# Expert results summed in PSUM, with one buffer for the rows of a block that VectorE transposes

## The chip, the cores and the metric

The kernel runs on one core of a Trainium2 chip, in float32. The metric is device time in microseconds (us) of one execution, the median of three runs.

## The reference

Two trunk layers, each a mixer (layer 0: retention and differential attention; layer 1: a Hyena convolution) followed by a mixture of experts, work on 384 tokens of 1024 channels (128 context tokens and 256 latent tokens). What matters here is the mixture of experts and the sum behind it:

```python
def moe_ffn(h, router_w, router_bias, w_gate, w_up, w_down):    # 16 experts, D_FF_EXPERT = 512
    scores = sigmoid(t @ router_w)                              # t: the tokens
    ...
    _, eidx = lax.top_k(jnp.where(emask, sel, -jnp.inf), TOP_K) # TOP_K = 2
    wsel = jnp.take_along_axis(scores, eidx, axis=-1)
    wsel = wsel / wsel.sum(-1, keepdims=True)
    ...
    act = jax.nn.silu(hg) * hu * comb[:, :, None].astype(t.dtype)
    return jnp.einsum('tef,efd->td', act, w_down).reshape(B, L, D)
...
    h = x * (1.0 + sc2) + sh2
    y = moe_ffn(h, ...)
    x = layer_norm(ALPHA * x + g2 * y, P['ln_w'][l, 1], P['ln_b'][l, 1])
```

## The kernel before

The 384 tokens are three tiles of 128. The router gives each token two experts, and each of the 768 pairs gets a slot. The slots of an expert fill blocks of 32 slot rows, so that an expert has one block or more; how many is known only at run time. GpSimd scatters the tokens' rows (1024 float32 each) into a table in DRAM, `slot_rows`, with six indirect DMAs.

A loop then goes over the 16 experts (`pe_moe`, experts with many and with few blocks mixed) and over each expert's blocks (`block_of_expert`). SyncE's queue streams the weights, three transfers of 2 MB for each expert (gate, up, down), in the order of the experts, into four pairs of buffers for gate and up and three for down; a buffer is filled again when the last block of its expert has read it. With two layers these are 96 transfers.

One block is this, by engine:

- TensorE: `gate_and_up` for eight groups of 128 channels (L954; the slot rows, transposed, are the stationary operand of 32 columns, and four matmuls fill the four groups of 32 columns of the array), then `rows_to_channels` (L947: four transposes of the **next** block's rows), then `down` for four groups of 128 hidden units (L961), which waits until VectorE has delivered the gated and transposed activation.
- ScalarE: silu of the gate (L1409); half of the down result from PSUM to SBUF (L1412), the other half by VectorE (L1546); then ScalarE's queue stores the block to `slot_rows` in two DMAs (L1417).
- VectorE: silu times up and the transpose, in two halves (L1529, L1531), the next block's rows from PSUM (L1524), the copy (L1546).
- GpSimd: it waits until the rows have landed in `slot_ahead[odd]` and until TensorE has transposed the last ones, copies them to `slot_in` (L575, L576) and issues the reads of the block after next into the buffer that has just come free (L566), two DMAs of 32 x 512 float32.

The first two blocks of a layer don't come from DRAM: a matmul with a 0/1 matrix picks them out of the tokens.

After the loop GpSimd gathers two rows for each token from `slot_rows` with six indirect DMAs, TensorE multiplies them by diagonal matrices of the routing weights and adds them (`pe_join` in layer 0, `pe_last` in layer 1), and VectorE adds the gated sum to the residual (`total`, in `dve_norm` and `dve_last`) and takes the statistics of the layer norm (L1286 and L1339). In layer 0 the matmuls of the next modulation (L633) stand ahead of the join on TensorE, and SyncE's first load of the Hyena weights waits for the gathers.

## Time and profile before

| | |
|---|---|
| runs | 1202.0, 1203.97 and 1207.95 us, median 1203.97 us |
| profiled execution | 1201.09 us, of which the span of the trace is 1199.4 us |
| mean granted TensorE clock | 0.951 |
| busy share of the span | PE 84%, PEld 47%, DVE 33%, ACT 20%, POOL 16% |
| read from and written to HBM | 320.02 MB, 23.63 MB |
| chain of work that ended last | PE 63%, DMA 21%, DVE 10% |

The span is the time from the first to the last instruction of the trace; the execution's own time has a little more around it. PE is TensorE's matmuls, PEld its loads of stationary operands, which run beside them; DVE is VectorE, ACT ScalarE, POOL GpSimd, and SP SyncE. The granted clock is a share of 2.4 GHz. In rows of the trace L954 is line 954 of the kernel, and "[0.54 <-DVE arena L1531]" means that the engine had been idle for 0.54 us until an instruction of VectorE at L1531 released it. A float32 matmul leaves two records, so 32 matmuls of `gate_and_up` appear as x64.

### The profile page before, as it was taken

To read this page: it belongs to the slowest core of one execution; us is meant where nothing else is said; L and a number is where in the kernel's file an instruction comes from. 1 tells how busy PE (TensorE), PEld (TensorE's weight loads), DVE (VectorE), ACT (ScalarE), POOL (GpSimd) and SP (SyncE) were. 2 spreads that over 40 slices of the span, in tenths; PEclk is the share of its full clock that TensorE was granted. 3 is DMA by queue.
4 is the path that set the end of the run, shared out by engine and by line. 5 is a ranking of instruction groups with operands and counts; after the bars stand their busy time and mean duration, and the time that the engine had idled before them with its cause. 6 is when DMAs were issued, how large, how long until landed. Compare 5 with 4: busy or idle time off the path is not lost.

```text
span 1199.4 us, 24149 instructions
## 1 busy us (share of the span) xinstructions
PE 1013.1 (84%) x9499; PEld 561.7 (47%) x9499; DVE 400.3 (33%) x1149; ACT 239.8 (20%) x507; POOL 190.9 (16%) x389
## 2 busy tenths in 40 slices
PE   4899998899769899795679999999978977998564
PEld 2344447654435455453345555455454544555231
DVE  0320115744612222121353533645552221222116
ACT  0401003631411121111131111210141121121102
POOL 0320000300032222122110001002004221222111
PEclk9999999899789999898889999999979998999988
DMA  8998232977589999999892314636765799899984
GB/s 354 324 343 299 95 126 97 350 298 317 222 302 396 388 407 393 397 399 394 305 377 99 140 71 143 243 123 241 292 256 211 270 391 408 337 395 393 394 349 158
DMA packets 76278, 344.62 MB, mean 287 GB/s; under 512 B 8883, under 2 KB 9011, under 8 KB 62900
## 3 DMA queue, kind: packets, MB, share of 16 engines
q1 hardware_dynamic: 54756, 291.40, 62.9%
q0 software_dynamic: 14512, 41.78, 10.2%
q10 hardware_dynamic: 6944, 10.49, 2.5%
q8 instruction: 49, 0.80, 0.3%
q14 instruction: 17, 0.14, 0.0%
HBM read 320.02 MB, written 23.63 MB: 287 GB/s over the span
## 4 chain that ended last, share of the span: by engine, by line
PE 63%; DMA 21%; DVE 10%; ACT 2%; issue 2%; SPq 1%; POOL 0%; POOLq 0%; ACTq 0%; DVEq 0%
PE bank L954 13%; PE bank L743 12%; PE bank L1019 11%; PE bank L961 7%; DMA ring<-in_moe_w_up_dram 7%; PE bank L872 7%; DMA ring<-in_ada_w_dram 3%; DMA ring<-in_moe_w_down_dram 3%; DMA arena<-in_moe_w_up_dram 3%; PE bank L633 3%; DMA ring<-in_ev_w_in_dram 3%; PE bank L1122 1%; PE bank L1098 1%; ACT arena L1409 1%; DVE arena L1531 1%
## 5 line engine op out<-in xcount | busy, mean ns | idle before, releaser
L954 PE MATMUL bank<-ring,arena 128*32 128x256 f32 x2496 | 149.9, 391 | 28.8 <-DMA ring<-in_moe_w_up_dram 25.7
L743 PE MATMUL bank<-ring,arena 128*128 128x512 f32 x336 | 146.7, 598 | 2.5 <-DMA ring<-in_ev_w_in_dram 2.5
L954 PE MATMUL bank<-arena 128*32 128x256 f32 x1792 | 108.1, 395 | 28.3 <-DMA arena<-in_moe_w_up_dram 28.3
L1019 PE MATMUL bank<-arena,ring 128*128 128x384 f32 x384 | 126.3, 492 | 1.9 <-issue 1.9
L1529 DVE TENSOR_TENSOR arena<-arena,bank 128x64 f32<-128x64 f32 x136 | 27.4, 201 | 296.2 <-ACT arena L1409 296.2
L954 PEld LDWEIGHTS bank<-ring,arena 128*32 128x32 f32 x2496 | 83.7, 113 | 88.5 <-issue 41.7
L961 PE MATMUL bank<-ring,arena 128*32 128x256 f32 x1440 | 87.0, 382 | 27.3 <-DVE arena L1531 22.2
L743 PEld LDWEIGHTS bank<-ring,arena 128*128 128x128 f32 x336 | 64.2, 192 | 82.9 <-issue 80.2
L1019 PEld LDWEIGHTS bank<-arena,ring 128*128 128x128 f32 x384 | 73.5, 192 | 54.4 <-issue 5.0
L954 PEld LDWEIGHTS bank<-arena 128*32 128x32 f32 x1792 | 60.3, 114 | 72.0 <-issue 39.4
L872 PE MATMUL bank<-ring,arena 128*128 128x512 f32 x192 | 83.2, 593 | 1.3 <-DVE arena L2096 1.3
L566 POOL DMA_DIRECT2D arena<-slot_rows x140 | 70.8, 506 | 60.6 <-POOL arena L576 43.5
L961 PEld LDWEIGHTS bank<-ring,arena 128*32 128x32 f32 x1440 | 42.9, 109 | 55.9 <-DVE arena L1531 33.2
L1412 ACT ACTIVATE arena<-bank 64x256 f32<-64x256 f32 x68 | 25.9, 381 | 181.8 <-PE bank L961 181.8
L1546 DVE COPY arena<-bank 64x256 f32<-64x256 f32 x68 | 28.3, 416 | 100.1 <-PE bank L961 100.1
L575 POOL TENSOR_TENSOR small<-small 128x1 f32<-128x1 f32 x66 | 12.4, 188 | 298.5 <-PE bank L947 291.5
L872 PEld LDWEIGHTS bank<-ring,arena 128*128 128x128 f32 x192 | 36.2, 190 | 45.7 <-issue 44.0
L1409 ACT ACTIVATE arena<-bank 128x128 f32<-128x128 f32 x68 | 18.8, 277 | 186.9 <-PE bank L954 185.7
L961 PE MATMUL bank<-arena 128*32 128x256 f32 x704 | 42.5, 382 | 14.3 <-DVE arena L1531 11.1
L1409 ACT ACT_TABLE_LOAD x34 | 43.6, 1283 | 47.2 <-issue 47.2
L633 PE MATMUL bank<-ring,small 128*32 128x256 f32 x640 | 39.4, 402 | 9.5 <-DMA ring<-in_ada_w_dram 9.5
L576 POOL COPY arena<-arena 64x512 f32<-64x512 f32 x66 | 39.6, 600 | 0.0
(367 smaller groups left out, 1074.9 us busy)
## 6 DMA issues: line engine op xcount, KB each, us to landing
ring<-in_ada_w_dram SPq DMA_DIRECT2D x24, 2048.0 KB, 13.4
ring<-in_moe_w_down_dram SPq DMA_DIRECT2D x20, 2048.0 KB, 23.5
ring<-in_moe_w_gate_dram SPq DMA_DIRECT2D x18, 2048.0 KB, 24.1
ring<-in_moe_w_up_dram SPq DMA_DIRECT2D x18, 2048.0 KB, 29.4
arena<-in_moe_w_gate_dram SPq DMA_DIRECT2D x14, 2048.0 KB, 26.7
arena<-in_moe_w_up_dram SPq DMA_DIRECT2D x14, 2048.0 KB, 31.9
arena<-in_moe_w_down_dram SPq DMA_DIRECT2D x12, 2048.0 KB, 20.1
ring<-in_ev_w_in_dram SPq DMA_DIRECT2D x7, 2048.0 KB, 19.4
```

What stands on the lines that cost most here:

```text
L566: pool.dma_start(slot_ahead[odd][h * BLK:(h + 1) * BLK, :], slots[bass.ds(block * BLK, BLK), h * 512:(h + 1) * 512]).then_inc(S[f"row_in{o ...
L576: pool.tensor_copy(slot_in, slot_ahead[odd]).then_inc(S["row_rdy"], 1)
L633: pe.matmul(b[32 * j:32 * j + 32, 0:HALF], condT[:, 2 * k:2 * k + 32], slot8(chunks[j // 2])[:, k, j % 2 * HALF:j % 2 * HALF + HALF], star ...
L743: last = pe.matmul(bank[3 * (c % 2) + t], hT[:, k, t * P:(t + 1) * P], slot8(n)[:, k, :], start=k == 0, stop=k == KT - 1)
L872: last = pe.matmul(bank[2 * t + half], src[:, k, t * P:(t + 1) * P], slot8(n0 + half)[:, k, :], start=k == 0, stop=k == KT - 1)
L954: last = pe.matmul(bank[1][q * BLK:(q + 1) * BLK, 0:HALF], slot_inT[:, k, :], both[:, :, k, q * P:(q + 1) * P], start=k == 0, stop=k == KT ...
L961: last = pe.matmul(bank[5][tile * BLK:(tile + 1) * BLK, 0:HALF], act_T[:, f, :], slot4(s + 2)[:, f, q * HALF:(q + 1) * HALF], start=f == 0 ...
L1019: last = pe.matmul(bank[c % 3][:, 0:T], slot8(n)[:, k, (c % 4) * P:(c % 4 + 1) * P], hT[:, k, :], start=k == 0, stop=k == KT - 1)
L1409: act.activation(silu_g, bank[1][:, 0:P].rearrange("p (r f) -> p f r", f=FT), ACT.Silu).then_inc(S["silu"], 1)
L1412: act.activation(slot_out[odd][:, HALF:2 * HALF], bank[5][2 * BLK:4 * BLK, 0:HALF], ACT.Copy).then_inc(S["evac_act"], 1)
L1529: dve.tensor_tensor(act_rows[:, two, :], silu_g[:, two, :], up, ALU.mult).then_inc(S["gated"], 1)
L1546: dve.tensor_copy(slot_out[odd][:, 0:HALF], bank[5][0:2 * BLK, 0:HALF]).then_inc(S["evac_dve"], 1)
```

## The change

The down results no longer go to DRAM. Six of the eight PSUM banks hold the sum for all 384 tokens and 1024 channels during the whole loop. After each block, twelve matmuls (`add_to_tokens`, three tiles of tokens by four quarters of the channels) add its 32 rows to the tokens they belong to. Their stationary operand `sel_w` is 32 slot rows by 128 tokens and holds the routing weight where the token has that slot, and 0 elsewhere; it is laid out four times, once for each group of 32 rows of the array, and VectorE makes it anew for each block from the tokens' slots and weights, which are spread over the partitions once per layer. The stores, the gathers, the diagonal matrices and the joining matmuls go, and so do some matmuls (`WARM`, `LAST_WARM`) whose result nobody read.

The rows of a block are read by one DMA of 32 x 1024 float32 into the one buffer `slot_ahead`. VectorE, not TensorE, transposes them, with four instructions of 32 x 256, and GpSimd issues the next read when these are done. The loops of VectorE, ScalarE and GpSimd go by single blocks instead of pairs. One block is picked by a matmul at the start of a layer, not two, and pushed through the array already transposed.

After layer 0's loop, VectorE's `total` reads the sums from PSUM, and the matmuls of the modulation are issued beside it; their columns are now taken up after `total` and `spread`. SyncE's first load of the Hyena weights no longer waits for gathers.

```diff
@@ pool_moe
-            rows_ahead(2, 0)
-            rows_ahead(3, 1)
-            with pool.Fori(1, pairs) as pair:
-                for odd in range(2):
-                    pool.wait_ge(S[f"row_in{odd}"], pair * 32)
-                    pool.wait_ge(S["rowT_mm"], pair * 2 + (odd + 1))
-                    pool.tensor_tensor(idle, wsel[:, 0, 0:1], wsel[:, 0, 0:1], ALU.add)
-                    pool.tensor_copy(slot_in, slot_ahead[odd]).then_inc(S["row_rdy"], 1)
-                    pool.wait_ge(S["row_rdy"], pair * 2 + (odd + 1))
-                    rows_ahead(pair * 2 + (odd + 2), odd)
+            def rows_in(block):
+                pool.dma_start(slot_ahead, slots[bass.ds(block * BLK, BLK), :]).then_inc(S["row_in"], 16)
+
+            rows_in(1)
+            with pool.Fori(2, blocks + 1) as b:
+                pool.wait_ge(S["rowT"], b)
+                rows_in(b)
...
-            for t in range(NT):
-                for r in range(2):
-                    pool.indirect_dma_start(picked[:, t, r, :], None, slots[:, :],
-                                            bass.IndirectOffsetOnAxis(ap=idx[:, r * NT + t:r * NT + t + 1], axis=0)).then_inc(gathered[t], 16)
@@ pe_moe
+            def add_to_tokens(turn, closing=False):
+
+                for t in range(NT):
+                    if t == 2:
+                        pe.wait_ge(S["first_added"], turn)
+                        pe.sem_inc(passed, 1)
+                    for q in range(4):
+                        rows = slice(q * BLK, (q + 1) * BLK)
+                        half = NT * q + t
+                        last = pe.matmul(joined[:, t, q, :], sel_w[rows, t * P:(t + 1) * P], slot_out[rows, :], start=False,
+                                         stop=closing and t > (half ^ 1) % NT)
+                    if t == 0:
+                        last.then_inc(S["first_added"], 1)
+                return last
+
             def block_of_expert(b, s):
 
                 pe.wait_ge(S["rowT"], b + 1)
                 for k in range(KT):
+                    if k == KT - 1:
+                        pe.wait_ge(S["evac_dve"], b + 1)
+                        pe.wait_ge(S["evac_act"], b + 1)
+                        pe.wait_ge(S["sel"], b + 1)
                     last = gate_and_up(s, k)
                 last.then_inc(S["gu_mm"], 1)
-                rows_to_channels()
+                add_to_tokens(b + 1)
                 pe.wait_ge(S["act"], b * 2 + 1)
-                pe.wait_ge(S["evac_dve"], b + 1)
-                pe.wait_ge(S["evac_act"], b + 1)
                 pe.wait_ge(*full(s + 2))
@@ act_moe
+            with act.Fori(0, blocks) as b:
+                act.wait_ge(S["gu_mm"], b + 1)
+                act.activation(silu_g, bank[0][:, 0:P].rearrange("p (r f) -> p f r", f=FT), ACT.Silu).then_inc(S["silu"], 1)
+                act.wait_ge(S["down_mm"], b + 1)
+                act.activation(slot_out[2 * BLK:4 * BLK, :], bank[1][2 * BLK:4 * BLK, 0:HALF], ACT.Copy).then_inc(S["evac_act"], 1)
@@ dve_moe
+            def rows_to_channels():
+                for g in range(4):
+                    last = dve.transpose(slot_inT[g * BLK:(g + 1) * BLK],
+                                         slot_ahead[:, g * HALF:(g + 1) * HALF].rearrange("s (i k) -> s k i", k=KT))
+                last.then_inc(S["rowT"], 1)
...
+            with dve.Fori(0, blocks) as b:
+                dve.wait_ge(S["silu"], b + 1)
+                gated(b, 0)
+                gated(b, 1)
+                dve.wait_ge(S["row_in"], b * 16 + 16)
+                rows_to_channels()
+                dve.wait_ge(S["down_mm"], b + 1)
+                dve.tensor_copy(slot_out[0:2 * BLK, :], bank[1][0:2 * BLK, 0:HALF]).then_inc(S["evac_dve"], 1)
+                for r, o in enumerate((sel_w, sel_w1)):
+                    last = dve.scalar_tensor_tensor(o, token_slot[:, r, :], block_slot, token_w[:, r, :], ALU.is_equal, ALU.mult)
+                last.then_inc(S["sel_step"], 1)
+                dve.wait_ge(S["sel_step"], b * 2 + 1)
+                dve.tensor_tensor(sel_w, sel_w, sel_w1, ALU.add).then_inc(S["sel"], 1)
@@ the order on TensorE after layer 0's experts
-            pe_ada(pe, 1, 1, bank[1])
             pe.wait_ge(ck_in, 64)
-            pe.transpose(bank[3][:, 0:2 * KT], ln_col_rows, ident[0:2 * KT, 0:2 * KT]).then_inc(hyc_mm, 1)
-            pe_ada_columns(pe, 1, 1, bank[1])
-            pe.wait_ge(scales_rdy, 1)
-            pe_join(pe, 0)
-            pe_join(pe, 1)
-            pe_join(pe, 2)
+            pe.transpose(bank[1][:, 0:2 * KT], ln_col_rows, ident[0:2 * KT, 0:2 * KT]).then_inc(hyc_mm, 1)
+            pe_ada(pe, 1, 1, bank[0])
+            pe.wait_ge(ln_var, NT)
             pe_norm_channels(pe, 0)
             pe_norm_channels(pe, 1)
+            pe_ada_columns(pe, 1, 1, bank[0])
             pe_norm_channels(pe, 2)
```

On GpSimd the queue around the start of a layer's loop and one turn of it read as follows before; the names in brackets are the semaphores that an instruction waits for.

```order
L566 DMA arena<-slot_rows 32x512 [waits scattered,order_ready]
L566 DMA arena<-slot_rows 32x512 x3
L571 UNCONDITIONAL_BRANCH
L571 ISA
L574 ISA [waits row_in0_0]
L575 ISA
L575 TENSOR_TENSOR small<-small 128x1 [waits rowT_mm_0]
L576 COPY arena<-arena 64x512
L566 ISA [waits row_rdy_0]
L566 DMA arena<-slot_rows 32x512
L566 ISA
L566 DMA arena<-slot_rows 32x512
```

The same place of the changed kernel:

```order
L564 DMA arena<-slot_rows 32x1024 [waits scattered,pick_mm,order_ready]
L567 UNCONDITIONAL_BRANCH
L564 ISA [waits rowT_0]
L564 DMA arena<-slot_rows 32x1024
L567 ISA
L567 COMPARE_AND_BRANCH
```

Before, four halves (two blocks) are issued ahead of the loop and the copy at L576 frees a buffer; now one read is issued ahead of it, and each further one waits for `rowT`, which VectorE's transposes raise.

On VectorE one block of the loop reads as follows before.

```order
L1529 TENSOR_TENSOR arena<-arena,bank 128x64
L1530 ISA
L1531 STREAM_TRANSPOSE arena<-arena 128x64
L1529 TENSOR_TENSOR arena<-arena,bank 128x64
L1530 REGISTER_ALU
L1531 STREAM_TRANSPOSE arena<-arena 128x64
L1542 REGISTER_ALU
L1524 COPY arena<-bank 128x256
L1545 ISA
L1546 COPY arena<-bank 64x256
L1539 REGISTER_ALU
```

The same place of the changed kernel, where the wait for the rows that have come from DRAM is at L1499:

```order
L1487 TENSOR_TENSOR small<-small,psum 128x64
L1488 ISA
L1489 STREAM_TRANSPOSE arena<-small 128x64
L1487 TENSOR_TENSOR small<-small,psum 128x64
L1488 REGISTER_ALU
L1489 STREAM_TRANSPOSE arena<-small 128x64
L1499 ISA
L1480 STREAM_TRANSPOSE arena<-arena 32x256 x4
L1502 COPY arena<-psum 64x256
L1504 SCALAR_TENSOR_TENSOR arena<-arena,small 128x384 x2
L1507 TENSOR_TENSOR arena<-arena 128x384
L1508 TENSOR_SCALAR small<-small 128x1
```

The copy of the transposed rows out of PSUM (L1524) has become four transposes, which stand between the gating and the copy of the down result, and the selection matrix for the block is made behind that copy.

## Rows read from the trace of the kernel before

**Rows 1.** The first line of the page.

```profile
span 1199.4 us, 24149 instructions
```

**Rows 2.** Busy time by stretch: engines, PEclk, DMA share, GB/s.

```profile
core 0: us, PE busy (x) PEld busy (x) DVE busy (x) ACT busy (x) POOL busy (x), PEclk, DMA share, GB/s
343.70:574.70 231.00, 189.91 (x3148) 107.84 (x3140) 48.94 (x191) 41.19 (x79) 57.12 (x131) 0.95 1.01 393
923.40:938.60 15.20, 13.59 (x240) 7.91 (x244) 4.19 (x17) 2.60 (x5) 5.09 (x12) 1.00 0.13 35
495.00:502.00 7.00, 6.74 (x67) 3.16 (x68) 0.00 (x0) 0.08 (x1) 0.00 (x0) 0.55 0.99 403
```

**Rows 3.** Timeline of one block: start us, us, instructions [idle before].

```profile
421.06 3.64 PE L954 MATMUL bank<-arena 128*32 128x256 f32 x64
...
424.63 0.46 PE L947 MATMUL bank<-keep,arena 64*128 64x64 f32 x4
...
425.63 1.93 PE L961 MATMUL bank<-ring,arena 128*32 128x256 f32 x32 [0.54 <-DVE arena L1531]
...
426.57 1.07 POOL L566 DMA_DIRECT2D arena<-slot_rows  x2 [0.66 <-POOL arena L576]
...
427.38 3.64 PE L954 MATMUL bank<-arena 128*32 128x256 f32 x64
```

**Rows 4.** Groups by line and form: busy us, mean ns | idle before.

```profile
L954 PE MATMUL bank<-ring,arena 128*32 128x256 f32 x2496 | 149.9, 391 | 28.8 <-DMA ring<-in_moe_w_up_dram 25.7 <-issue 3.1
L954 PE MATMUL bank<-arena 128*32 128x256 f32 x1792 | 108.1, 395 | 28.3 <-DMA arena<-in_moe_w_up_dram 28.3
...
L1531 DVE STREAM_TRANSPOSE arena<-arena 128x64 f32<-128x64 f32 x136 | 33.4, 246 | 4.7
...
L1524 DVE COPY arena<-bank 128x256 f32<-128x256 f32 x70 | 27.0, 386 | 5.3 <-PE bank L947 2.7 <-issue 2.6
...
L1988 DVE SCALAR_TENSOR_TENSOR arena<-arena,small 128x384 f32<-128x384 f32 x8 | 4.9, 618 | 0.3
```

**Rows 5.** Timeline at 781 us: full matmuls of 256 columns in layer 1.

```profile
780.88 1.89 PE L1098 MATMUL bank<-arena 128*128 128x256 f32 x8
...
782.61 0.38 PE L1093 MATMUL bank<-arena 128*128 128x128 f32 x2
```

**Rows 6.** Timeline at 234 us: attention scores on groups of 64 rows.

```profile
234.27 0.71 PE L813 MATMUL bank<-arena 64*128 64x256 f32 x4
...
234.81 0.40 PE L814 MATMUL bank<-arena 64*128 64x128 f32 x4
```

**Rows 7.** Line L566 from 410 to 440 us: its transfers' landings.

```profile
DMA to landing us min/median/max: 5.8/6.8/7.8
```

**Rows 8.** Line L566, one pair; first its first transfer alone, then both.

```profile
DMA to landing us min/median/max: 5.9/5.9/5.9
...
L566 POOL DMA_DIRECT2D arena<-slot_rows x2: 496/504/512, 432.9 to 433.5; - x2
...
DMA to landing us min/median/max: 5.9/6.5/7.1
```

**Rows 9.** Line L566 from 1163 to 1170 us, after the last weights.

```profile
DMA to landing us min/median/max: 2.1/2.2/2.3
```

**Rows 10.** DMA queues from 420 to 460 us: packets, MB, share of 16 engines.

```profile
q1 hardware_dynamic: 987, 14.34, 89.5%
...
q10 hardware_dynamic: 633, 0.87, 6.0%
```

**Rows 11.** Timeline of POOL at 911 us, the start of layer 1's reads.

```profile
911.28 2.09 POOL L566 DMA_DIRECT2D arena<-slot_rows  x4 [4.30 <-DMA slot_rows<-arena,idx]
```

**Rows 12.** Timeline at the end: last down matmuls, last statistics.

```profile
1162.46 1.93 PE L961 MATMUL bank<-ring,arena 128*32 128x256 f32 x32 [0.55 <-DVE arena L1531]
...
1188.26 0.21 DVE L1339 BATCH_NORM_AGGREGATE small<-small 128x2 f32<-128x12 f32 x1
```

**Rows 13.** Timeline after layer 0's experts: modulation, last statistics.

```profile
584.19 6.50 PE L633 MATMUL bank<-ring,small 128*32 128x256 f32 x64 [9.54 <-DMA ring<-in_ada_w_dram]
...
606.33 0.21 DVE L1286 BATCH_NORM_AGGREGATE small<-small 128x2 f32<-128x12 f32 x1
```

More of the change, by code:

```diff
@@ L385, in trunk_program @@
         idle = tiny(1)
+        block_slot = tiny(1)
         warm = tiny(1)
@@ L584, in pool_moe @@
             if l == 0:
+                pool.wait_ge(S["down_mm"], before_last)
+                pool.tensor_tensor(idle, eps_col, eps_col, ALU.add).then_inc(pool_chain, 1)
+                pool.wait_ge(pool_chain, 2)
                 norm_gate_rows(pool)
-            for odd in range(2):
-                pool.wait_ge(S[f"row_in{odd}"], pairs * 32)
-            pool.wait_ge(S["stored0"], stores * 32 + 32)
-            pool.wait_ge(S["stored1"], odd_stores * 32 + 32)
-            pool.wait_ge(S["rowT"], blocks + 1)
@@ new lines, in act_moe @@
+            last.then_inc(spread_act, 1)
+            act.wait_ge(spread_mm, 2 * l + 2)
+            for r in range(2):
+                last = act.activation(token_slot[:, r, :], bank[1 + r][:, 0:T], ACT.Copy)
+            last.then_inc(spread_act, 1)
+            act.wait_ge(table_rdy, l + 1)
+            act.sem_inc(S["evac_act"], 1)
+            blocks = act.value_load(table[0:1, NE:NE + 1], min_val=NE, max_val=MAX_BLOCKS)
+            with act.Fori(0, blocks) as b:
[3 more added lines that the diff above has]
+                act.activation(slot_out[2 * BLK:4 * BLK, :], bank[1][2 * BLK:4 * BLK, 0:HALF], ACT.Copy).then_inc(S["evac_act"], 1)
@@ L1532, in gated @@
                               act_rows[:, two, :].rearrange("p f s -> p (f s)")).then_inc(S["act"], 1)
[L1534 to L1546 removed]
+            dve.wait_ge(pick_mm, l + 1)
```

286 lines of the change are left out of this document (106 added, 180 removed).

## The prediction

> **What bounds the kernel now.** I read the span first and the chain of work (63% TensorE, 21% transfers, 10% VectorE, in the table above), then stretches of the two expert loops, then one block, then the landings of its row reads. The span is 1199.4 us of a profiled execution of 1201.09 us; the median of the runs is 1203.97 us, so a difference worked out in the trace is added to 1204 [rows 1]. A change under 0.5% (6 us) is about what a measurement of this kernel cannot tell from none.
>
> The change lives in the two expert loops. From the fourth expert's weights on, layer 0 takes from 343.7 to 574.7 us, and its DMA share is 1.01 at 393 GB/s: the weight stream never rests. Layer 1 is the same from 938.6 us on, but in the 15 us before that the DMA share is 0.13: all buffers were full and TensorE was the slower one [rows 2]. So the two are close. A block costs TensorE 6.32 us (421.06 to 427.38): 3.57 us of gate and up, then 1.00 us in which it transposes the next rows and waits for silu and gating, then 1.75 us of down [rows 3]. The count of gate and up matmuls (4288, 64 to a block) gives 67 blocks, 33 in layer 0 and 34 in layer 1; ahead of these matmuls TensorE also idles 54 us for weights in both loops [rows 4]. The 31 blocks of layer 0 that lie in the stage are 196 us of its 231.
>
> **What the change does to a block.** On TensorE the four transposes go and twelve matmuls of 32 rows by 128 columns, moving 256 columns, come in. Each float32 matmul is two records; eight records of 256 columns take 1.73 us, 0.22 us each [rows 5]. One after another the 24 would take 5.2 us. But they sit on four groups of 32 rows. The nearest row is the attention scores: four records of 256 columns on two groups of 64 rows, and the next ones start 0.54 us later, where 0.87 us would be due in line [rows 6]. With four groups side by side I take 24 / 4 * 0.22 = 1.3 us, and 0.2 us to fill: 1.5 us. This hides the wait for silu, so TensorE's block becomes 3.5 + 1.5 + 1.8 = 6.8 us. Below: no less than the 1.0 us gap that is there now (6.3 us); above: 5.2 us in line (10.5 us).
>
> The Trainium skill (TensorE: Matmul & The Clock Gate, Part 3) gives 3.07 times for four row tiles of 32. By it the 24 records are an estimated 1.7 us and the block 7.0 us. No run here shows four groups of rows yet.
>
> The row transfer is what I worry about. Before, there are two buffers, one for even and one for odd blocks; each is filled two blocks ahead, and a copy on GpSimd frees it, so a landing of 7 us is hidden. After, there is one buffer. GpSimd issues the read of block b+2 only when VectorE has transposed block b+1, and VectorE transposes block b+2 only when it has landed. This ring has four terms:
> - semaphore to issue on GpSimd: 0.66 us, as after its copy now [rows 3];
> - issue to landing. While the weight stream runs, a 64 KB half takes 5.8 to 7.8 us, median 6.8 [rows 7]. Of the pair issued at 432.9 and 433.5 us the first half took 5.9 us and the second 7.1 us, so 7.7 us from the first issue [rows 8]. The new transfer is both halves in one, 32 runs of 4 KB. Between 5.8 (the second half rides free) and 7.7 I take the middle, 6.7 us;
> - VectorE's start, an estimated 0.1 us;
> - four transposes of 32 x 256. The transpose of 64 columns is 0.25 us, a copy of 256 columns 0.39 us, a two-operand instruction of 384 columns 0.62 us [rows 4]. I take the copy, 4 * 0.39 = 1.55 us; ends 1.0 and 2.2 us.
>
> Sum: 0.66 + 6.7 + 0.1 + 1.55 = 9.0 us for each block that runs beside weight loads. With nothing else in flight a half lands in 2.1 to 2.3 us [rows 9], the ring takes 4.6 us or so, and TensorE's 6.8 us decide.
>
> The rest of VectorE's new work follows the transposes: a copy of 0.39 us and three two-operand instructions of 384 columns, 0.62 us each at most, with hops 2.4 us [rows 4]. TensorE wants it at the eighth of eight gate and up steps, 7/8 of 3.57 = 3.1 us after the transposes. Hidden, with 0.7 us to spare; if it is late, it adds its lateness to every block. ScalarE loses its stores; its table load comes in each block now, while TensorE does gate and up: hidden, and if it weren't, the wait for silu would grow beneath the 1.5 us of summing.
>
> Waiting behind VectorE's wait for the rows: its copy of the down result, so the summing and the next gate and up. Nothing overtakes it.
>
> **The loops, worked out.** The stores leave the DMA engines: 6.0% of their time beside 89.5% of weights [rows 10]. 2 MB of weights, now 5.9 us (14.34 MB in 40 us), then take 5.6 us. Of a layer's 48 transfers ten have landed when the stage starts (three experts and one matrix), so 38 remain, 213 us. Layer 0: two blocks are done by then, and the third waits for its last matrices, to about 351 us; the 206 us to the end of the weights hold 23 blocks at 9.0, and the other 8 at 6.8 are 54 us: end at 611 against 574.7, +36. Layer 1: only one block is picked on TensorE now, so the second waits for its read, issued as now at 911.3 us [rows 11], to 915 us; 213 us beside weights hold 24 blocks, 9 more take 61 us: end at 1189 against 1164.4, +25. Experts of one block (9 us) still outrun their weights (3 * 5.6 = 17 us); of the 54 us of such idling I leave 10 us (0 to 20). Loops: **+71 us**.
>
> **The joins.** Stores, gathers and scaled matmuls go. Layer 1: from the last down matmul's end, 1164.4 us, to the end of the statistics, 1188.5 us, are 24.1 us [rows 12]. After: 2.4 us for the selection, 1.5 us of summing, 0.1 us, then VectorE's twelve passes over 512 columns, an estimated 0.7 us each (0.62 us for 384 columns [rows 4]), and the statistics, 10.2 us, all in line: 14.2 us. Gain 10 us. Layer 0: 574.7 to 606.5 us are 31.9 us, of which the matmuls of the modulation (584.19 us on) hold back the join [rows 13]; after, they run beside VectorE. 4.0 + 11.8 us, 1 us for the moved scale columns, and some 2 us because the gate rows, issued one block before the end, land later than they are wanted: gain 13 us. Joins: **-23 us**.
>
> What is before the loop: the pick turns into 48 records that load 128 columns, but the rows of the second block are later than that anyway. GpSimd still issues six scatters; nothing is queued ahead of the reads.
>
> Sum: 1204 + 71 - 23 = 1252; I say **1250 us**. With 5.8 us and transposes of 1.0 us the ring is 7.5 us: the loops +1 and the 10 us, total 1192. With 7.7 and 2.2 us it is 10.6 us: loops +117, total 1298.
>
> **Rivals.**
> - *The reads are hidden and the kernel is faster.* Without stores the landings shrink. It decides at a landing of 4.5 us: then the ring is 6.8 us, TensorE's own. The loops end with the weights: layer 0 at 343.7 + 213 + 5 = 562 us (-13), layer 1 about as now. Total 1204 - 13 - 23 = **1168**. For it: 2.2 us when idle [rows 9], and the stores were in flight beside most reads. Against it: the stores were 6% of the engines' time, and no loaded read is under 5.8 us.
>   The Trainium skill (DMA: Bandwidth & Descriptors, Queues, rings and completion order) says that each DMA engine takes turns between queues, packet by packet. A weight packet of 14.5 KB keeps an engine 0.58 us by the trace (987 of them in 89.5% of 40 us of 16 engines); the two row packets per engine of a transfer would wait two such turns, 2.2 + 1.2 = 3.4 us, an estimate by that rule, and this rival would hold. The trace disagrees: a half has 32 runs too, and takes 5.9 us [rows 8].
> - *The row groups run in line.* TensorE's block is 10.5 us, whatever the rows do: 31 blocks from 351 (+102), 33 from 915 (+97): **1380 us**. Against it: [rows 6].
> - *The clock.* TensorE would idle 2.2 us in each 9.0. With gaps of 0.54 us in every block [rows 3] the granted clock is 0.95 of 2.4 GHz over the stage, and in the 7 us after one of the long waits for weights it is 0.55, about 1.2 GHz, though TensorE is busy [rows 2]. If it fell so in a third of the 47 blocks beside weights, each of them would last 4 us longer: +60, about **1300 us** or a little over.
>
> **Chances.** Forecast 0.72, hidden 0.12, in line 0.04, clock 0.07, something else 0.05. Range 1190 to 1300: it leaves out the hidden and the in-line case and some of the rest, 2 in 10. Faster: the hidden case and the low edge of the forecast, 0.16; same 0.05; slower 0.79.
>
> **What would show it.** Right: VectorE's idle time ahead of the four transposes is the largest in the loop and put down to the row transfer; it lands 6 to 7.5 us after issue beside weights; TensorE's block is 9 us there and 6.8 elsewhere; the DMA share in layer 0's loop falls under 0.9. The twelve matmuls take 1.5 us. Wrong: landings under 4.5 us, or a stage whose share stays at 1.0.

## The result: slower by 12%

The changed kernel takes 1347.38 us (median of 1346.27 to 1351.8), against 1205.96 us for the kernel before in the same comparison: ratio 1.1182, 95% interval 1.1136 to 1.1227. The prediction was 1250 us, 1190 to 1300. The direction was right and the size was not: 141 us were lost where 46 were forecast. The profiled execution has a span of 1344.6 us, 145.2 us more than before [rows 1].

The page of the changed kernel, its head, part of the chain of work, and groups by line:

```profile
span 1344.6 us, 26543 instructions
PE 1127.6 (84%) x10919; PEld 632.7 (47%) x10919; DVE 652.2 (49%) x1594; ACT 278.7 (21%) x540; POOL 92.7 (7%) x169
...
PE 48%; DMA 25%; DVE 21%; issue 4%; ACT 2%; POOLq 0%; SPq 0%; DVEq 0%
...
L1480 DVE STREAM_TRANSPOSE arena<-arena 32x256 f32<-32x256 f32 x268 | 168.1, 627 | 104.5 <-DMA arena<-slot_rows 101.8
L920 PE MATMUL psum<-ring,arena 128*32 128x256 f32 x2496 | 161.8, 417 | 63.2 <-DVE arena L1480 63.2
L920 PE MATMUL psum<-arena 128*32 128x256 f32 x1792 | 127.6, 448 | 63.1 <-DVE arena L1480 63.1
...
L1378 ACT ACT_TABLE_LOAD x67 | 86.0, 1283 | 1.6 <-issue 0.4
```

TensorE's matmuls have the same busy share as before, which says nothing. Look at who is waited for. Before, gate and up waited for weights only [rows 4]. Now they wait 63.2 us and, in the other group of L920, 63.1 us for VectorE's transposes, and those wait 101.8 us for the row reads. Neither group of gate and up names weights any more. A transpose of 32 x 256 takes 0.627 us, where 0.39 was forecast.

The stage of layer 0, in the very window of [rows 2], shows where the weight stream went (columns as there):

```profile
343.70:574.70 231.00, 186.32 (x2864) 100.69 (x2856) 124.72 (x303) 45.13 (x71) 11.28 (x23) 0.91 0.76 286
```

The DMA share is 0.76 at 286 GB/s, where it was 1.01 at 393. The chain that ended last, piece by piece in this stage (start us, us, what), is the ring itself, with TensorE nowhere in it:

```profile
421.06 7.58 DMA arena<-slot_rows
...
428.67 0.62 DVE arena L1480
429.30 0.62 DVE arena L1480
429.94 0.63 DVE arena L1480
430.58 0.64 DVE arena L1480
431.24 0.05 POOLq L564
...
431.35 0.48 issue
```

Issue 0.6, landing 7.6 and transposes 2.55 add up to 10.8 us for this block. The timeline from 441 us on has one block of each kind:

```profile
431.26 6.20 PE L920 MATMUL psum<-ring,arena 128*32 128x256 f32 x64 [3.72 <-DVE arena L1480]
...
441.31 3.66 PE L920 MATMUL psum<-arena 128*32 128x256 f32 x64 [0.46 <-DVE arena L1480]
...
441.90 0.49 POOL L564 DMA_DIRECT2D arena<-slot_rows  x1 [9.56 <-DVE arena L1480]
...
444.90 1.61 PE L940 MATMUL psum<-arena 32*128 32x256 f32 x24
...
446.44 1.93 PE L927 MATMUL psum<-ring,arena 128*32 128x256 f32 x32
448.44 0.38 ACT L1380 ACTIVATE arena<-psum 64x256 f32<-64x256 f32 x1 [3.12 <-PE psum L927]
...
449.77 2.54 DVE L1480 STREAM_TRANSPOSE arena<-arena 32x256 f32<-32x256 f32 x4 [3.53 <-DMA arena<-slot_rows]
```

The block that starts at 441.31 is done on TensorE at 448.4, but its successor's rows, asked for at 441.90, land at 449.7, and gate and up start at 452.4: 11.05 us. The block before it ran its gate and up at a granted clock of 0.58 (6.20 us for 64 matmul records) and cost nothing, since the read was out as long. The summing of L940 begins at 444.90 and down at 446.44: 1.54 us, as forecast.

Of 67 reads 44 landed beside weights, after 5.8 to 8.7 us, median 7.4; 19 landed alone, after 2.5 us, and then a block lasts 7.45 us, not 6.8; the other four lie between. Those alone fall in pauses of the weight stream, since a buffer is filled again only when the last block of its expert has read it: in layer 0 no weights land from 527.2 to 555.0 us and from 598.5 to 629.9 us, and the last of them lands at 646.3 us. Before, none is more than 8 us behind the one ahead of it from 352.0 us on, and the last lands at 572.6 us. Ahead of the loop the pick has grown. Here is the kernel before:

```profile
327.76 2.78 PE L939 MATMUL bank<-arena 128*32 128x512 f32 x24 [1.95 <-DVE arena L1509]
332.28 1.93 PE L954 MATMUL bank<-ring,arena 128*32 128x256 f32 x32 [0.52 <-issue]
```

and the changed one, with its last down matmuls and last statistics of each layer:

```profile
328.27 11.52 PE L910 MATMUL psum<-arena 128*128 128x32 f32 x48
...
341.59 3.67 PE L920 MATMUL psum<-ring,arena 128*32 128x256 f32 x40
...
657.33 1.93 PE L927 MATMUL psum<-ring,arena 128*32 128x256 f32 x32
...
678.15 0.21 DVE L1249 BATCH_NORM_AGGREGATE small<-small 128x2 f32<-128x12 f32 x1
...
990.01 1.51 PE L920 MATMUL psum<-ring,arena 128*32 128x256 f32 x12
...
1313.91 1.93 PE L927 MATMUL psum<-ring,arena 128*32 128x256 f32 x32
...
1320.81 2.94 PE L940 MATMUL psum<-arena 32*128 32x256 f32 x24 [4.97 <-DVE arena L1507]
...
1333.44 0.21 DVE L1308 BATCH_NORM_AGGREGATE small<-small 128x2 f32<-128x12 f32 x1
```

From these and [rows 12, 13], and the first gate matmul of layer 1 before (905.02 us): layer 0's loop took 242.4 us and takes 317.7 (+75), layer 1's took 259.4 and takes 325.8 (+66); the start of each is some 10 us later, counted from the routing ahead of it, by the pick; the time from the last down to the last statistics falls from 31.9 to 19.1 us in layer 0 (-13) and from 24.1 to 17.8 in layer 1 (-6). The rest is 3 us between the layers. That is +142 +20 -19 +3 us, which is all of the 145 us but for rounding.

### The profile page after: what moved, and what is told of

Same layout as the page of the kernel before. It is cut to its first block, busy times and chain, and to the rows that moved or that the text cites. A ratio compares the mean times of both kernels' runs of the same rounds, so it can differ in the third digit from the quotient of the medians.

```text
span 1344.6 us, 26543 instructions
## 1 busy us (share of the span) xinstructions
PE 1127.6 (84%) x10919; PEld 632.7 (47%) x10919; DVE 652.2 (49%) x1594; ACT 278.7 (21%) x540; POOL 92.7 (7%) x169
## 3 DMA queue, kind: packets, MB, share of 16 engines
q0 software_dynamic: 11520, 35.09, 8.1%
## 4 chain that ended last, share of the span: by engine, by line
PE 48%; DMA 25%; DVE 21%; issue 4%; ACT 2%; POOLq 0%; SPq 0%; DVEq 0%
DMA arena<-slot_rows 23%; DVE arena L1480 13%; PE psum L698 11%; PE psum L998 9%; PE psum L920 8%; PE psum L827 6%; DMA ring<-in_ev_w_in_dram 2%; PE psum L612 2%; PE psum L910 2%; PE psum L1101 1%; PE psum L891 1%; PE psum L1077 1%; DVE small L1487 1%; DVE small L1931 1%; PE psum L1097 1%
## 5 line engine op out<-in xcount | busy, mean ns | idle before, releaser
L1480 DVE STREAM_TRANSPOSE arena<-arena 32x256 f32<-32x256 f32 x268 | 168.1, 627 | 104.5 <-DMA arena<-slot_rows 101.8
L920 PE MATMUL psum<-ring,arena 128*32 128x256 f32 x2496 | 161.8, 417 | 63.2 <-DVE arena L1480 63.2
L920 PE MATMUL psum<-arena 128*32 128x256 f32 x1792 | 127.6, 448 | 63.1 <-DVE arena L1480 63.1
L920 PEld LDWEIGHTS psum<-ring,arena 128*32 128x32 f32 x2496 | 83.2, 120 | 143.8 <-DVE arena L1480 81.0
L698 PE MATMUL psum<-ring,arena 128*128 128x512 f32 x336 | 146.7, 598 | 2.4 <-DMA ring<-in_ev_w_in_dram 2.4
L998 PE MATMUL psum<-arena,ring 128*128 128x384 f32 x384 | 126.5, 492 | 5.3 <-issue 5.3
L920 PEld LDWEIGHTS psum<-arena 128*32 128x32 f32 x1792 | 64.2, 128 | 126.5 <-DVE arena L1480 76.5
L940 PE MATMUL psum<-arena 32*128 32x256 f32 x1656 | 113.6, 403 | 9.2 <-DVE arena L1507 9.2
L1487 DVE TENSOR_TENSOR small<-small,psum 128x64 f32<-128x64 f32 x134 | 27.0, 201 | 180.6 <-ACT small L1378 180.6
L698 PEld LDWEIGHTS psum<-ring,arena 128*128 128x128 f32 x336 | 64.1, 192 | 82.9 <-issue 80.3
L940 PEld LDWEIGHTS psum<-arena 32*128 32x128 f32 x1656 | 75.4, 187 | 47.6 <-issue 37.7
L927 PE MATMUL psum<-ring,arena 128*32 128x256 f32 x1440 | 87.0, 382 | 0.0
L827 PE MATMUL psum<-ring,arena 128*128 128x512 f32 x192 | 83.2, 593 | 1.3 <-DVE arena L2051 1.3
L1504 DVE SCALAR_TENSOR_TENSOR arena<-arena,small 128x384 f32<-128x384 f32 x134 | 75.7, 602 | 0.0
L927 PEld LDWEIGHTS psum<-ring,arena 128*32 128x32 f32 x1440 | 42.2, 109 | 38.1 <-DVE arena L1489 14.9
L827 PEld LDWEIGHTS psum<-ring,arena 128*128 128x128 f32 x192 | 36.2, 190 | 45.7 <-issue 44.0
```

Source lines behind the costliest of these rows:

```text
L698: last = pe.matmul(bank[3 * (c % 2) + t], hT[:, k, t * P:(t + 1) * P], slot8(n)[:, k, :], start=k == 0, stop=k == KT - 1)
L827: last = pe.matmul(bank[2 * t + half], src[:, k, t * P:(t + 1) * P], slot8(n0 + half)[:, k, :], start=k == 0, stop=k == KT - 1)
L920: last = pe.matmul(bank[0][q * BLK:(q + 1) * BLK, 0:HALF], slot_inT[:, k, :], both[:, :, k, q * P:(q + 1) * P], start=k == 0, stop=k == KT ...
L927: last = pe.matmul(bank[1][q * BLK:(q + 1) * BLK, 0:HALF], act_T[:, f, :], slot4(s + 2)[:, f, q * HALF:(q + 1) * HALF], start=f == 0, stop ...
L940: last = pe.matmul(joined[:, t, q, :], sel_w[rows, t * P:(t + 1) * P], slot_out[rows, :], start=False, stop=closing and t > (half ^ 1) % NT)
L998: last = pe.matmul(bank[c % 3][:, 0:T], slot8(n)[:, k, (c % 4) * P:(c % 4 + 1) * P], hT[:, k, :], start=k == 0, stop=k == KT - 1)
```

## The experiments

Every ratio is against the kernel before, run beside it.

Four of the kernels leave work out, so layer 1 gets other values than the reference's and routes them otherwise. They run 66 blocks, 33 in each layer, where the changed kernel runs 67. The line for gate and up in the kernel without reads has 1728 records where the changed kernel's has 1792, and 64 are one block:

```profile
L917 PE MATMUL psum<-arena 128*32 128x256 f32 x1728 | 100.5, 385 | 14.0 <-DVE arena L1477 9.6
```

Layer 0 has the same 33 blocks in all of them and can be compared as it is. From the start of its first gate and up to the start of its last it takes 234.4 us in the kernel before and 310.6 us in the changed one.

**No reads.** The reads of a loop and the wait for them go; VectorE transposes the second block's rows each time, so the values of the later blocks are not the reference's.

```diff
             rows_in(1)
-            with pool.Fori(2, blocks + 1) as b:
-                pool.wait_ge(S["rowT"], b)
-                rows_in(b)
...
-                dve.wait_ge(S["row_in"], b * 16 + 16)
+                dve.wait_ge(S["row_in"], 16)
```

> Every row read after the first of a layer is left out, with the wait for it; VectorE transposes the same rows again for each block. Theory (the ring of one buffer: read, transposes, read): no block lasts longer than the 7.45 us of the blocks without weight loads, the loops shorten by up to 46 x 3.1 = 140 us and give some 20 us back as waits for weights, so about 1225 us. Rival (the twelve summing matmuls are the cost): they are all still there, so it stays above 1300 us.

Measured: 1199.71 us, ratio 0.9978 (0.9847 to 1.0108). All but five blocks last 7.44 to 7.45 us, and layer 0 takes 239.6 us, 71 less than in the changed kernel and 5 more than before. So without the reads the loss is gone, although all the summing matmuls are there; the block that layer 1 lacks is up to 7 us of the whole time. The waits for weights that I expected back came to under 10 us, so my 1225 was too high.

**No sums in the loop.** `add_to_tokens(b + 1)` is left out of `block_of_expert`, and the wait in the last twelve is set to fit.

> The twelve summing matmuls of each block are left out; only the last twelve, behind the loop, remain. Theory (the ring): nothing changes, within 10 us of 1347 us, since TensorE only waits longer for the transposed rows. Rival (the summing is the cost): 67 x 1.6 = 107 us less, about 1240 us.

Measured: 1328.76 us, 1.0985 (1.0904 to 1.1066). 19 us less, not 107. The theory said within 10 us, and the missing block of layer 1, some 10 us long, is about what it misses by: layer 0 takes 309.8 us against 310.6. In the changed kernel the summing is hidden.

**A quarter of each row.**

```diff
-                rows_in(b)
+                pool.dma_start(slot_ahead[:, 0:256], slots[bass.ds(b * BLK, BLK), 0:256]).then_inc(S["row_in"], 16)
```

> From the third block of a layer on, each read brings a quarter of a row (32 runs of 1 KB, not of 4 KB); the rest of the buffer keeps the second block's rows. If a read waits for turns behind weight packets, 32 runs wait as before, and it lands beside weights after 6 to 7 us, time 1310 to 1345 us. If its bytes cost, it lands after 3 to 4 us and the time is about 1260 us.

Measured: 1289.37 us, 1.0659 (1.0565 to 1.0754). Between 400 and 480 us these reads land after 6.0 us (median) and the full ones after 7.1. A quarter of the bytes saves 1.1 us, so bytes are a small part, and the landing is what the first theory said. The time is not: 58 us less, below its 1310. Layer 0 gained 27 us (283.8 against 310.6), about 1.1 us in each of its blocks beside weights; the rest is layer 1's, the missing block included.

**ScalarE issues the reads.**

```diff
             with act.Fori(0, blocks) as b:
+                act.wait_ge(S["rowT"], b + 1)
+                act.dma_start(slot_ahead, slots[bass.ds((b + 1) * BLK, BLK), :]).then_inc(S["row_in"], 16)
                 act.wait_ge(S["gu_mm"], b + 1)
```

> ScalarE issues the row reads instead of GpSimd, at the same point (after the block's transposes). If the landing is a matter of waiting behind weight packets, it stays at 6.5 to 7.5 us and the time within 20 us of 1347 us. Rival (GpSimd's way of issuing costs the time): 3 to 4 us to land beside weights, about 1240 us.

Measured: 1326.96 us, 1.097 (1.0913 to 1.1028); landings in the same stretch 6.9 us. That is 20 us less in time and nearly the same landing: GpSimd's queue is not the cause.

**Two buffers.** As in the kernel before, each read goes out two blocks ahead; the single transfer and the four transposes stay.

```diff
...
+            rows_in(1, 1)
+            rows_in(2, 0)
...
+            with pool.Fori(1, pairs) as p:
+                for k in range(2):
+                    pool.wait_ge(S["rowT"], p * 2 + k)
+                    rows_in(p * 2 + (1 + k), 1 - k)
...
```

> Two row buffers, each read issued two blocks ahead when VectorE has transposed its former rows; the last one or two blocks of a layer use one of them. Theory: landings of 7.4 us are hidden, every block takes 7.45 us as without reads, so 1200 to 1215 us. Rival (the reads cost by what they take from the weight stream, not by the wait for them): above 1260 us.

Measured: 1217.99 us, 1.0123 (1.0102 to 1.0144). Landings are still 7.2 us, but blocks last 7.45 and 7.6 us in turn. It is 15 us above the kernel before where the changed kernel is 141 above: one more buffer brings back some 127 us.

**One transpose for four.** One buffer again, with a row's quarters on four partition groups.

```diff
-                pool.dma_start(slot_ahead, slots[bass.ds(block * BLK, BLK), :])
+                pool.dma_start(slot_ahead, slots[bass.ds(block * BLK, BLK), :].rearrange("s (g c) -> g s c", g=4))
...
-                for g in range(4):
-                    last = dve.transpose(slot_inT[g * BLK:(g + 1) * BLK],
-                                         slot_ahead[:, g * HALF:(g + 1) * HALF].rearrange("s (i k) -> s k i", k=KT))
+                dve.transpose(slot_inT, slot_ahead.rearrange("p (i k) -> p k i", k=KT)).then_inc(S["rowT"], 1)
```

> One buffer as in the changed kernel, but a row's four quarters go to four groups of 32 partitions (128 runs of 1 KB), so that one VectorE transpose of 128 x 256 does the work of four of 32 x 256. Theory: a transpose costs by its columns, 0.65 us, 1.95 us less in the ring: 8.6 us beside weights if the landing stays at 7.4 us, TensorE's 7.0 us elsewhere, about 1250 us. Rival (four times as many runs land later, by 2 us or more): 1330 us or above.

Measured: 1349.67 us, 1.119 (1.1122 to 1.1259): the rival's outcome. The group and the chain of this kernel (start us, us, what) show both halves:

```profile
L1479 DVE STREAM_TRANSPOSE arena<-arena 128x256 f32<-128x256 f32 x67 | 41.6, 621 | 174.3 <-DMA arena<-slot_rows 174.3
```

```profile
410.67 11.73 DMA arena<-slot_rows
```

A transpose costs by its columns: 0.62 us for 128 rows as for 32. But the read lands after 11.7 us instead of 7.1, which eats it up. Blocks away from weights last 6.86 us, TensorE's own length.

**Both, and then the pick as rows.** The second kernel also picks the first block by twelve matmuls with `pick` as the stationary operand, on four groups of 32 columns, and one transpose out of PSUM.

> Both: two buffers and one transpose. Theory: neither the landing nor the transposes are on TensorE's path any more; a block takes 7.0 us (3.6 of gate and up, 1.55 of summing, 1.85 of down), 67 x 0.45 = 30 us less than with two buffers alone, about 1175 us, and 5 to 15 us more where weights are waited for.

> As before, and the first block of a layer is picked as rows: twelve matmuls with the pick as the stationary operand on four groups of 32 columns, then one VectorE transpose out of PSUM. Theory: the pick takes 1.5 us instead of 11.5 us, and the weight stream, which waits for it, starts 9 us earlier in each layer, so 15 to 18 us less than without, about 1160 us. Rival (the second block waits for its row read anyway, so the pick is hidden): no difference.

Measured: 1217.04 us, 1.0113 (1.009 to 1.0137), and 1209.75 us, 1.006 (1.003 to 1.009). Most blocks last 6.86 us, but no time was gained over two buffers alone: reads that land after 12.2 us are late again in places, and the last experts wait 9 us and more for weights. I expected 1175 and 1160 us. The pick is worth 7 us by the medians, half of what I expected, and the two intervals just touch; alone, in the changed kernel:

> The changed kernel with the first block of a layer picked as rows, nothing else. Theory: the pick (11.5 us) delays the start of the loop and of the fourth expert's weights in each layer, so 8 us in each, about 1330 us. Rival (the second block waits for its row read and its weights anyway): within 5 us of 1347 us.

Measured: 1335.66 us, 1.1103 (1.1049 to 1.1157). That is 12 us less by the medians, but the interval overlaps the changed kernel's, so the size is only roughly known. The traces show the step: layer 0's first gate and up starts at 330.8 us instead of 341.6, and the second block's at 343.6 instead of 350.4.

**Weights in short runs.** Each 2 MB transfer of weights becomes four, with runs of 4 KB; here, and where the weights are cut by partitions, the semaphore that tells of their landing counts four times as far.

```diff
-            sp.dma_start(dst, src).then_inc(ring_full[SLOT[s + j]], 16)
+            few = rows // P // 4
+            for part in range(4):
+                sp.dma_start(dst[:, part * few:(part + 1) * few], src[:, part * few:(part + 1) * few]).then_inc(ring_full[SLOT[s + j]], 16)
```

> The changed kernel with each 2 MB weight transfer issued as four of 0.5 MB, whose runs are 4 KB and not 16 KB; bytes and order stay the same. Theory (a row read waits for turns behind weight packets, each as long as its packet): packets of a quarter make its landing beside weights 3 to 4.5 us instead of 7.4, most blocks then last 7.45 us, and the time is 1210 to 1260 us. Rival (the read waits for a fixed amount of queued bytes, or for shared bandwidth): the landing stays above 6 us and the time above 1320 us.

Measured: 1294.68 us, 1.0755 (1.0692 to 1.0817); landings 5.6 us. The row read does depend on what the weights' transfers look like, but less than I expected; neither account had it, and the time, too, lies between their two.

**Two partition groups.** A row in two halves, two transposes of 64 x 256. First as one transfer of 64 runs, then as two of 32:

```diff
-                pool.dma_start(slot_ahead[odd], slots[bass.ds(block * BLK, BLK), :].rearrange("s (h c) -> h s c", h=2)).then_inc(S["row_in2" if tail else f"row_in{odd}"], 16)
+                for h in range(2):
+                    pool.dma_start(slot_ahead[odd][h * BLK:(h + 1) * BLK],
+                                   slots[bass.ds(block * BLK, BLK), h * 512:(h + 1) * 512]).then_inc(S["row_in2" if tail else f"row_in{odd}"], 16)
```

> Two buffers and the pick as rows, with a row in two halves on two groups of 32 partitions (64 runs of 2 KB) and two VectorE transposes of 64 x 256; the rows' quarters are stored in the order that this needs. Theory: landings beside weights of 8 to 9 us are hidden (128 runs took up to 12), transposes of 1.3 us still end before the down result, so blocks last 6.86 us as with one transpose and fewer packets take turns with the weights: 1195 to 1208 us. Rival (only TensorE's work and the weights decide): 1210 us as with one transpose.

> Two buffers, the pick as rows and two transposes of 64 x 256, but each block's rows come as two transfers of 32 runs of 2 KB, not as one of 64 runs. The one transfer left 272 packets in the trace, a transfer of 32 runs leaves 48. Theory (a read's landing beside weights grows with its packets, which take turns with weight packets): 96 packets land after 8 to 9 us, hidden by two buffers, blocks last 6.86 us, 1195 to 1208 us. Rival (two partition groups are slow in themselves): 1300 us as with the one transfer of 64 runs.

Measured: 1315.65 us, 1.0907 (1.0838 to 1.0976), and 1183.26 us, **0.9815 (0.9784 to 0.9846)**: 132 us between two ways to write the same copy. I had both wrong, the first by over 100 us and the second by 12 us, since it came out below its range. The lines of the DMA queue of GpSimd (packets, MB, share), first of the changed kernel, then of the kernel with one transpose, of the one transfer of 64 runs and of the two of 32:

```profile
q0 software_dynamic: 11520, 35.09, 8.1%
```

```profile
q0 software_dynamic: 17952, 35.20, 8.1%
```

```profile
q0 software_dynamic: 26528, 35.21, 8.7%
```

```profile
q0 software_dynamic: 12592, 35.10, 8.9%
```

The MB are equal, the packets are not. The kernel without reads leaves 8400 packets with two reads in it, so a read of the changed kernel is (11520 - 8400) / 65 = 48 packets; the four-group read is 144, the 64-run read 272, and the pair of halves 64 in all, not the 96 that I expected. The line on packet sizes, in the same order, shows which they are:

```profile
DMA packets 66761, 329.08 MB, mean 245 GB/s; under 512 B 5347, under 2 KB 5475, under 8 KB 53380
```

```profile
DMA packets 73193, 329.17 MB, mean 244 GB/s; under 512 B 11780, under 2 KB 11908, under 8 KB 59813
```

```profile
DMA packets 81770, 329.20 MB, mean 251 GB/s; under 512 B 20356, under 2 KB 20484, under 8 KB 68389
```

```profile
DMA packets 67833, 329.08 MB, mean 277 GB/s; under 512 B 6419, under 2 KB 6547, under 8 KB 54452
```

Packets of 512 B and more number 61414 in three of them and 61413 in the fourth. All that the other ways of writing the copy add are packets under 512 B: 96, 224 and 16 for each read.

The median landings between 400 and 480 us are 7.1, 11.7 (12.2 in the kernel with two buffers), 16.3 and, for one of the two halves, 6.4 us; a pair lands 7.6 us (median) after the issue of its first half. With the quarter read, which leaves (10448 - 8400) / 64 = 32 packets and lands after 6.0 us, the order of the landings is the order of the packets. The last kernel's block, in steady state beside the weights:

```profile
429.65 3.64 PE L934 MATMUL psum<-arena 128*32 128x256 f32 x64
...
434.48 1.26 DVE L1494 STREAM_TRANSPOSE arena<-arena 64x256 f32<-64x256 f32 x2
434.76 1.93 PE L941 MATMUL psum<-ring,arena 128*32 128x256 f32 x32
...
436.39 1.08 POOL L565 DMA_DIRECT2D arena<-slot_rows  x2 [5.62 <-DVE arena L1494]
436.51 3.64 PE L934 MATMUL psum<-arena 128*32 128x256 f32 x64
```

and its window over layer 0's loop (columns as in [rows 2]):

```profile
343.00:565.00 222.00, 220.56 (x3788) 130.49 (x3788) 132.90 (x348) 60.09 (x93) 32.63 (x65) 0.99 1.00 380
```

The transposes have no idle time ahead of them and end before down does; TensorE is busy for 220.56 of 222 us at a granted clock of 0.99, with the DMA share at 1.00. This version is faster than both kernels; than the one before it by 1.9%, an interval that excludes no change but not a gain under 2%.

**Two buffers, one transpose and the pick as rows, without the sums.** The twelve matmuls of each block are left out.

> The kernel with two buffers, one transpose and the pick as rows, without the twelve summing matmuls of each block (the last twelve stay). Here TensorE's block of 6.86 us is the bound, so leaving them out shows what they cost: a block falls by 0.5 to 0.6 us (the 1.54 us of summing less the wait for silu and gating that it covers), which is up to 35 us, less what is then waited for weights: 1180 to 1195 us. Rival (the weights are the bound by now): 1205 us or above.

Measured: 1211.3 us, 1.0061 (1.0037 to 1.0084): no difference, the rival's outcome. The shortest blocks fall from 6.86 to 6.32 us and the time goes into waits for rows and weights; layer 0, from its first to its last gate and up, takes 245.9 us against 246.8. In that kernel, then, the sums cost about nothing; in the one with the halves I did not try it.

**The kernel before, reading one block ahead.**

```diff
             rows_ahead(2, 0)
-            rows_ahead(3, 1)
...
-                    rows_ahead(pair * 2 + (odd + 2), odd)
+                    rows_ahead(pair * 2 + (odd + 1), 1 - odd)
```

> The kernel before with one edit: GpSimd reads a block's rows one block ahead, not two, so that only one read is in flight. TensorE still transposes, and results still go through DRAM. Theory (the ring): issue 0.7 us, landing of the second half 7.7 us, copy 0.8 us make 9.2 us for a block beside weights instead of 6.3; some 45 such blocks, less half of the 54 us of weight waits, give 1290 us. Rival (the reads were hidden by more than the second buffer, and the loss of the change lies in VectorE's transposes): below 1230 us.

Measured: 1261.15 us, 1.0472 (1.0433 to 1.051). The loss appears without any other part of the change, at 57 us, two thirds of what I expected: many blocks lie between 6.3 and 11 us, and the waits for weights absorb more. So one read in flight is enough to lose by. The changed kernel loses more than twice as much, with transposes of 2.5 us in its ring where this one has a copy of 0.6 us, and with the pick; how the difference divides between them no run shows.

**Weights cut by partitions.**

```diff
-            sp.dma_start(dst, src).then_inc(ring_full[SLOT[s + j]], 16)
+            for part in range(4):
+                some = slice(part * 32, (part + 1) * 32)
+                sp.dma_start(dst[some], src[some]).then_inc(ring_full[SLOT[s + j]], 16)
```

> The changed kernel with each 2 MB weight transfer cut by partitions into four of 0.5 MB; the runs stay 16 KB, so each DMA engine gets two runs of each transfer, not eight. Theory A (an engine serves a whole turn of several weight runs before it turns to the row read, and a turn ends with a transfer): a turn shrinks from 8 x 0.58 = 4.7 us to 1.2 us, the landing from 7.1 to 3.6 us, the time is about 1220 us. Theory B (a turn holds a number of runs, whatever transfer they belong to): nothing changes, 7.1 us and 1335 to 1350 us; the 5.6 us of the transfers cut into runs of 4 KB then come from the shorter runs.

Measured: 1604.42 us, 1.3319 (1.315 to 1.3489). Neither: with transfers to 32 partitions each, all queues together move 218 GB/s between 440 and 480 us, with the DMA engines busy with weights for 96% of the time. A run of 16 KB then keeps an engine about 1.2 us instead of 0.65 (busy time of 16 engines in 40 us by the runs of 16 KB in the bytes moved), and a row read lands after 10.3 us. That is no 3.6 us, so a turn does not end with a transfer (theory A falls). 2.4 us plus 6.5 runs of 1.2 us are 10.3; 2.4 plus 7.2 of 0.65 are 7.1.

## Why the prediction was wrong

The mechanism was the one on record: one buffer, a ring of issue, landing and transposes, TensorE and the weights both waiting for it. What failed is the size of its terms, above all the transposes, and one term, the pick, that was put at nothing. Worked out below, the ring is 66 us of the 97 between 1250 and 1347, the blocks away from weights 12, the pick 20, the joins 4 and the stretch between the layers 3, less 10 us of waits for weights that were forecast and did not come: 95 in all.

- **Issue 0.66 us.** Right: 0.6 us.
- **Landing 6.7 us.** 7.4 us (median). "The middle" of 5.8 and 7.7 was a choice without a ground; the transfer is nearly the late end. Worth 0.7 us in 44 blocks, 31 us.
- **Transposes 1.55 us.** This is the step that failed worst: 2.5 us, 0.627 us each, beyond my upper end of 2.2. I took a copy of 256 columns as the nearest row, though the transposes of [rows 4] show 0.246 us for 64 columns, more than half a copy of 256. With the landing this makes the ring 10.5 us instead of 9.0; 44 blocks by 1.5 us are 66 us.
- **6.8 us where no weights run.** TensorE's own length is right (6.86 us where the transposes are short). But VectorE does gating first and then 2.5 us of transposes, which end some 0.4 us after down (0.46 in the row at 441.31). I checked VectorE's work against TensorE's only behind the transposes, not ahead of them: 7.45 us, 20 blocks by 0.6 us.
- **23 and 24 blocks beside weights.** 47 forecast, 44 seen, and that it is so near is luck. I divided a stream of 38 transfers without a pause (206 and 213 us) by the ring, and put all other blocks behind it. By that rule the measured ring of 10.5 us gives 40 blocks. The stream did pause, with a DMA share of 0.76, layer 0's last weights landed at 646.3 us and not at 557, and the blocks without weights lie in the pauses. The 10 us of waits for weights did not come: no group of gate and up names them.
- **Twelve matmuls in 1.5 us.** 1.54 us. Row groups side by side, as [rows 6] had suggested for two groups. The rival of groups in line falls: 24 records of 0.22 us in line would be 5.2 us, 3.4 times as long. The Trainium skill's 3.07 times for four row tiles (TensorE: Matmul & The Clock Gate, Part 3) is near it.
- **The pick, costed at nothing.** 11.5 us in place of 2.8, and 10 us later into the loop in each layer. The cover that I named, the second block's read, is there but too short: with the pick as rows layer 0's first block starts 10.8 us earlier and the second still 6.8. Of the fourth expert's weights, `up`, which waits for the first read, is issued at 343.1 us against 341.1 with the pick as rows (343.7 before), and `down`, which waits for a buffer that the first blocks free, at 350.0 against 342.3. Undoing the pick gives some 12 us back in the changed kernel.
- **Joins -23 us.** -13 us in layer 0, exactly; -6 instead of -10 in layer 1, because VectorE's last turn waits for the rows of a block that doesn't exist and transposes them before it copies the down result (TensorE idle for 4.97 us), and the last sums run at a granted clock of 0.57 (2.94 us for the 24 records).
- **Clock.** The granted clock fell to 0.926 over the span, and 22 blocks did their gate and up in 5.0 to 6.5 us instead of 3.66, at a granted clock of 0.55 to 0.73. With the reads gone it is 0.964. It cost little, since a slow block hides beneath its read; only four of them, whose rows came early, lasted 9.1 us instead of 7.45.
- **The signs.** Right were the twelve matmuls, the DMA share under 0.9, and most landings (7.4 us, some up to 8.7). Wrong were two: blocks last 9.6 to 12 us beside weights, not 9, and the idle time ahead of the transposes (104.5 us) is not VectorE's largest in the loop, since it waits 180.6 us for silu ahead of the gating.
- **Hidden reads, the faster rival.** Its point of decision was a landing of 4.5 us. None beside weights came near; but with a second buffer and few packets it holds, at 1183 us against the 1168 worked out for it.

The range failed with them. Its upper end had the ring that came, 10.6 us a block, and was sized at 1298 us. (Redone from its own terms, the loops come to +112 us and not +117, or to +122 with the 10 us of waits for weights: 1293 or 1303 us.) About 50 us lie beyond it: 25 more in the loops, some 13 of them in blocks away from weights and the rest because 44 blocks and not 40 met weights, 20 of pick, 4 in the joins and 3 between the layers.

I also read a rule of the Trainium skill wrongly. The Trainium skill (DMA: Bandwidth & Descriptors, Queues, rings and completion order) says that a DMA engine drains a whole packet of roughly 9 to 17 descriptors before it turns to another queue. I took a packet for one run of weights, and called the rule refuted. If a turn is instead the eight runs of a 2 MB transfer that fall to each engine, a little under the nine of that rule, a small read takes 2.4 + 8 * 0.65 = 7.6 us, which is near the 7.1 measured (0.65 us is a run of 16 KB; the prediction's 0.58 us was a mean that took in the queue's short packets). With 17 runs it would be 13.5 us, and nothing in the trace is like that for a read of 32 runs. Reads of 144 and 272 packets land one and two such turns of eight later (12 and 16.3 us). This account is argued from the numbers; no run shows a turn by itself, and neither the short weight runs (5.6 us) nor the runs of 1.2 us (10.3 us, where eight would give 12.0) fit a turn of eight. What ends a turn stays open.

## What to carry to other kernels

A buffer that is refilled only when its reader is done makes a ring: add issue, landing **under load** and the reader's time, and compare the sum with the period of the loop before removing a second buffer. An operation that seems hidden should be checked on both sides: what runs ahead of it on its own engine, and what waits for its end. And when data is spread over more partitions to please an engine, look at the packets that the transfer leaves in the trace, the small ones above all: here two plain transfers landed in less than half the time of the single one that was cut into 64 runs.

## What the chip showed that I had not expected

- A VectorE transpose has one price for 32, 64 or 128 partitions: some 0.63 us for 256 columns (0.246 us for 64 columns).
- One transfer of 64 runs of 2 KB to two groups of 32 partitions leaves 272 packets, 240 of them under 512 B, and lands after 16 us beside weights; two transfers of 32 such runs leave 64 and have both landed after 7.6 us.
- With weight transfers to 32 partitions at a time all queues together moved 218 GB/s, with those to 128 partitions 393 [rows 2].
- 48 matmul records whose stationary operand is 128 x 128 with columns 8 apart take 11.5 us, 0.24 us each, though they move only 32 columns.
